# Squares of the scan's outputs made inside its last group, heads of z scaled ahead, and a held low half behind the gating

## The chip, the cores and the metric

The kernel runs on one core of a Trainium2 chip. The metric is device time in microseconds. The core's engines are TensorE (PE; its weight loads are shown apart as PEld), VectorE (DVE), ScalarE (ACT), GpSimd (POOL) and SyncE (SP). Each works through its own instructions in order, and they wait for each other on semaphores. SP issues all weight loads.

## The reference

The program is a chain of layers on 272 tokens (16 meta tokens and 256 of the input; 48 places of padding in front count for nothing). What matters here is the gated delta rule of the first layer, cut to its skeleton:

```python
qkv = silu(causal_conv(h @ w_in[:, :4096]))      # q and k: 8 heads of 128, v: 16 heads of 128
z = h @ w_in[:, 4096:6144]                       # 16 heads of 128
# chunkwise scan over the tokens, per head: o = S^T q, S decays and takes in k v^T
o = o * rsqrt(mean(o * o, -1) + eps) * norm_w    # one factor per head and token
o = o * silu(z)
mix = o.reshape(L, 2048) @ w_out
```

Behind it stand the layer's feed-forward network, a second layer (mLSTM and feed-forward), and a second block with attention over the tokens and over a memory; the change doesn't touch them.

## The kernel before

All activations are held with features on the 128 partitions and tokens along the row: a head is a tile of 128 x 272 floats. A product of the split kind is made of three fp32r matmuls for each block of 128 x 128 weights (`L432` high weights by high input, `L433` high by low, `L434` low by high). For this, each slab of weights (128 x 2048, 1 MB) in `ring` is taken apart into `w_hi`, a rounded copy by ACT (`L302`), and `w_lo`, the rest, by DVE (`L305`). `ring` has four slots, `w_hi` and `w_lo` two. ACT may round slab n + 2 when PE has finished slab n; DVE follows; then SP may load slab n + 6's place, the slot just emptied (the load of a slab waits for `w_lo` of the slab four before it). `each_product` writes these steps into the order of an engine: for the unit j of a phase it issues the split (`ahead`) for each slab that ends with this unit, then the unit's `body`, then `late` for unit j - lag; after the last unit it runs `late` for the remaining ones. With `end="hold"` the split of the last slab is left out there, and a call of `prepare` makes it later.

**The scan.** The 16 value heads are worked through in four groups of four, each with tokens in two chunks. A group is a chain of levels (l = 1 to 5, then a last one): PE multiplies 64 x 64 blocks, DVE masks and subtracts, ACT copies one product of each chunk (`L1366`, at the last level `L1371`). Then come values, state and outputs. ACT copies the outputs of chunk 1 (`o1`) and chunk 2 (`outputs(2)`, which counts `group_out`) into `qkv[:, 16:32, :]` (`L1383`). In the first three groups ACT, DVE, PE and POOL also make the next group's inputs between these steps; in the last group there are none. The rows that POOL fetches for the groups (`bc`) and the squares of the outputs (`osq`) lie in the same memory, so squares can be written only when POOL has done its work for the last group (`ahead_pool`).

**Between scan and z.** ACT waits for the whole scan (`scan_done`), squares all 16 heads with one instruction (`L609`), makes `w_hi` of z's first two slabs, and the high halves of the input in eight steps (`L483`). DVE makes the two `w_lo`, then the eight low halves (`L491`). PE sums the squares over the partitions in `rown_pe` (`L636`, 16 blocks, each a matmul with one column of ones; in fp32, so two passes each) and goes on with z. ACT takes the root (`L620`), DVE the reciprocal (`L625`), POOL writes the 16 rows to memory and reads them back on all partitions (`obc`, `L1523`, `L1525`).

**z.** 8 slabs with two units (heads) each. ACT: `Silu` of the product into one of four tiles `zs` (`L1531`), and four units later the high half of the gated head (`L1537`). DVE: two units behind the product, the scaling of the head with `obc` (`L1547`), its gating with `zs` (`L1550`), and from unit 5 on at odd units the low half of a pair of heads (`L1559`):

```python
if un.u % 2 and un.u >= 5:
    low(un.u // 2 - 2)
```

`low(6)` and `low(7)` stand behind the phase. `x_lo` counts the pairs, and PE, which starts `gdn_out` right behind z, waits for pair k // 2 before block k. `gdn_out` has 8 slabs of 16 blocks, one product each. Behind the last gate POOL fetches `mem0`, squares and sums it (`L1957`, `L1960`) for a product that PE makes ahead of slab 5 of `gdn_out`.

The semaphore `rown_squares` counts squares of three uses: 16 of the keys and queries, 1 for the outputs, 2 of the memory's.

Of the kernel before, what the change touches and what calls it, by code (L numbers as in the profile page):

```python
# [19 lines left out]
ALU = mybir.AluOpType  # L20
# [8 lines left out]
T = META + SEQ  # L29
TILES = [(0, META), (META, P), (META + P, P)]  # L30
HQ, HV = 8, 16
# [169 lines left out]
def program(nc, x_t, meta_t, mem_t, positions, stream, consts, params, sg_w_t, sg_bias, out_t, counts):  # L201
    with ExitStack() as ctx:
# [424 lines left out]
        def rown_pe(pe, use, sqr, blocks, per_row, n, rows):  # L627
            S.begin("rown_pe")
            if use == 3:
                pe.wait_ge(*S.at("mla_act", "ksq"))  # L630
            else:
                pe.wait_ge(S.sem("rown_squares"), (16, 17, 19)[use])
            for k in range(blocks):
                src = sqr(k)
                h = k // per_row
                mm = pe.matmul(ps[5 if use == 3 else 4][0:rows, 0:n], cn("row_of", 15 - h, rows)[0:src.shape[0], :], src,  # L636
                               start=(k == 0), stop=(k == blocks - 1))
            S.inc(mm, "rown_pe", "sums")
# [3 lines left out]
        qkv = area(0, 32, T)  # L642
# [711 lines left out]
        def nothing_more():  # L1354
            pass

        def group_act(act, g, last):
            inc = lambda ins, step=None: S.inc(ins, "scan_act", step)
            S.begin("scan_act")
            for c in CHUNKS:  # L1360
                ahead_values_act(act, g, c)
            for l in range(1, TOP):
                for c in CHUNKS:
                    act.wait_ge(*S.at("scan_pe", f"XT{c}.{l}", g))
                    if l < TOP - 1:
                        inc(act.activation(XT64[c], packed(bank(c, 1)), ACT.Copy), f"XT{c}.{l}")  # L1366
                    else:
                        if g == 0 and c == 1:
                            act.wait_ge(*S.at("first_zeros"))
                        for s in HALVES:  # L1370
                            inc(act.activation(buf[c]["XT"][s, :, s], packed(bank(c, 1))[s], ACT.Copy), f"XT{c}.{l}" if s.start else None)  # L1371
                if l in (3, 4) and not last:
                    ahead_exp(act, g + 1, l - 2)

            def new_values(c):
                act.wait_ge(*S.at("scan_pe", f"vn{c}", g))
                inc(act.activation(buf[c]["vn"], tile4(bank(c, 1)), ACT.Copy), f"vn{c}")

            def outputs(c):
                t0, n = TILES[c]  # L1380
                act.wait_ge(*S.at("scan_pe", f"o{c}", g))
                dst = work[:, 16 * T:32 * T].rearrange("p (g h t) -> p g h t", h=4, t=T)[:, g, :, t0:t0 + n]
                return act.activation(dst, tile4(bank(c, 2)), ACT.Copy)  # L1383
            new_values(1)
            inc(outputs(1), "o1")
            new_values(2)
            if not last:
                ahead_x_act(act, g + 1, 1)
            outputs(2).then_inc(S.sem("group_out"), 1)
            if not last:  # L1390
                ahead_x_act(act, g + 1, 2)
# [148 lines left out]
            each_product(act, "gdn_z", 1, body, split="hi", late=high, lag=4, turns=0)  # L1540

        def gate_dve(dve):
            def body(un):
                S.begin("gate_dve")
                dve.wait_ge(S.sem("o_rows_in"), 16)
                o = qkv[:, 16 + un.u, :]
                S.inc(dve.scalar_tensor_tensor(out=o, in0=o, scalar=pm("gdn_norm"), in1=obc[:, un.u, :], op0=ALU.mult, op1=ALU.mult), "gate_dve")  # L1547
                S.own(dve, "gate_dve", un.u + 4)
                un.was_read(dve)
                S.inc(dve.tensor_tensor(o, o, zs[:, un.j % 4, :], ALU.mult), "gate_dve")  # L1550
                if un.u % 2 and un.u >= 5:
# [2 lines left out]
            def low(pair):  # L1554
# [2 lines left out]
                dve.wait_ge(*S.at("x_hi", pair, 2))  # L1557
                k = slice(2 * pair, 2 * pair + 2)
                S.inc(dve.tensor_tensor(O_LO[:, k, :], qkv[:, 16 + 2 * pair:18 + 2 * pair, :], O_HI[:, k, :].bitcast(F32), ALU.subtract), "x_lo", pair)  # L1559
            each_product(dve, "gdn_z", 1, nothing, split="lo", late=body, lag=2, turns=0)  # L1560
            low(6)
            low(7)

# [1076 lines left out]
        def _(act):  # L2640
# [21 lines left out]
            act.wait_ge(*S.at("qkv_act", turn=31 + CONV_AHEAD))  # L2662
            scan_act(act)
            scan_done(act)
            rown_squares(act, [(qkv[:, 16:32, :], osq)])
            prepare(act, "hi", "gdn_z")
            split_act(act, 1, a, A_HI, 8, T)
            rown_act(act, 1, [], T, 16, 1.0 / P, cn("eps"))
# [77 lines left out]
        def _(dve):  # L2746
# [5 lines left out]
            dve.memset(raw_c[:, :, 0:3], 0.0).then_inc(S.sem("qkv_dve"), CONV_AHEAD * 3)  # L2752
            dve.memset(rs[:, 0, 16:20], 0.0).then_inc(S.sem("qkv_act"), CONV_AHEAD)
            dve.memset(rs[:, 0, 20:24], 0.0).then_inc(S.sem("up_dve"), 2 * 4)
            dve.memset(rs[:, 0, 32:36], 0.0).then_inc(S.sem("gate_dve"), 4 * 2)
            dve.memset(rs[:, 0, 36:40], 0.0).then_inc(S.sem("hid_pool"), 4 * 2)
            dve.memset(rs[:, 0, 24:28], 0.0).then_inc(S.sem("up_act"), 2)
            dve.memset(rs[:, 0, 28:32], 0.0).then_inc(S.sem("up_pool"), 2 * 3)
# [2 lines left out]
                dve.wait_ge(bank_free[i], 1)  # L2761
            dve.wait_ge(S.sem("up_pool"), 6)
            dve.wait_ge(S.sem("qkv_act"), CONV_AHEAD)
            dve.wait_ge(S.sem("gate_dve"), 8)
            dve.wait_ge(S.sem("hid_pool"), 8)
            dve.wait_ge(S.sem("up_act"), 2)
            dve.wait_ge(S.sem("up_dve"), 8)
# [23 lines left out]
            split_dve(dve, 1, a, A_HI, A_LO, 8, T)  # L2791
            rown_dve(dve, 1, T, 16)
            gate_dve(dve)
            each_product(dve, "gdn_out", 1, lambda un: mem_norm_dve(dve, un.j), turns=0, split="lo", end="hold")
            for layer in range(2):
                if layer:
# [69 lines left out]
        def _(pe):  # L2866
# [7 lines left out]
            def gates_block(k):  # L2874
# [8 lines left out]
                if k == DB - 1:  # L2883
# [6 lines left out]
            stream_pe(pe, "gdn_qkv", a_parts(0, T), T, lead=1, between=lambda slab: qkv_pe(pe, 2 * slab),  # L2890
                      inside=lambda slab, part: qkv_pe(pe, 2 * slab + part))
            scan_pe(pe)
            pe.wait_ge(S.sem("group_out"), GROUPS + 1)
            rown_pe(pe, 1, lambda k: osq[:, k, :], 16, 1, T, 16)
            stream_pe(pe, "gdn_z", a_parts(1, T), T)
            stream_pe(pe, "gdn_out", split_input(pe, O_HI, O_LO, T, by_step(pe, 2, per=2)), T,
                      between=lambda slab: mem_norm_pe(pe) if slab == 5 else None)
# [231 lines left out]
```

## Time and profile before

| | |
|---|---|
| median of 3 runs | 1634.16 us (1631.63 to 1638.73) |
| the profiled execution | 1625.85 us, its span 1624.0 us |
| PE busy | 1556.2 us (96%) |
| DVE, ACT, POOL busy | 1064.9, 798.7, 373.5 us |
| mean granted clock of TensorE | 0.987 |

The busy times are of the profiled execution. PE is nearly always busy, so the stretches in which it isn't, and what ended them, are what to look for; the granted clock is 1.00 at full speed and 0.50 at the lower level.

### The profile page before, as it was taken

The page shows a single profiled execution, that of the slowest core. Times are in us where ns is not written, and L with a number is a line of the kernel's source. Part 1 is how long each engine was busy: PE and PEld are TensorE (multiplying, and loading weights), DVE is VectorE, ACT ScalarE, POOL GpSimd, SP SyncE. Part 2 cuts the span into 40 slices and gives each one's busy share as a digit, 9 for nine tenths or more (in the row PEclk, how much of TensorE's full clock was granted, in tenths as well). Part 3 has the DMA queues.
Part 4 walks back from the last instruction along what each step waited for, and adds up shares of the span by engine and source line. Part 5 has one row for each costly group of instructions (what it writes and reads, how often), then busy time and mean ns, then how long its engine had stood idle before and what let it go on. Part 6 is the DMA issues. An engine that isn't in the chain of part 4 may idle for free.

```text
span 1624.0 us, 33710 instructions
## 1 busy us (share of the span) xinstructions
PE 1556.2 (96%) x13961; PEld 1476.5 (91%) x13961; DVE 1064.9 (66%) x1531; ACT 798.7 (49%) x1202; POOL 373.5 (23%) x387
## 2 busy tenths in 40 slices
PE   6999999889899999999999999999999898899998
PEld 6898988789899998988999999999996798899998
DVE  6785465474888736665888557665557665666653
ACT  7764333554555546545655554434444246364332
POOL 0014442006266520003366311220000000212110
PEclk9999999999999999999999999999999999999999
DMA  7463220354555455623454556545633532545553
GB/s 271 156 196 94 51 60 2 134 185 165 184 179 181 143 169 180 210 93 125 161 181 157 178 198 207 203 148 192 230 113 119 208 129 93 194 160 203 175 169 122
DMA packets 43373, 256.47 MB, mean 158 GB/s; under 512 B 5712, under 2 KB 7872, under 8 KB 20992
## 3 DMA queue, kind: packets, MB, share of 16 engines
q1 hardware_dynamic: 38704, 233.26, 41.9%
q0 software_dynamic: 4416, 20.60, 4.4%
q8 instruction: 81, 1.33, 0.3%
q10 hardware_dynamic: 144, 1.05, 0.2%
q14 instruction: 28, 0.23, 0.0%
HBM read 252.68 MB, written 2.22 MB: 157 GB/s over the span
## 4 chain that ended last, share of the span: by engine, by line
PE 77%; DVE 8%; issue 7%; ACT 5%; DMA 2%; POOL 0%; ACTq 0%; SPq 0%; DVEq 0%; POOLq 0%
PE bank L432 21%; PE bank L434 21%; PE bank L433 21%; PE bank L1259 3%; DVE w_lo L305 2%; ACT w_hi L302 2%; DMA sq<-rows_scratch_q 1%; ACT work L2490 1%; DVE rs L589 1%; PE bank L636 1%; DVE mix L595 1%; DVE w_spare L1332 1%; PE bank L1429 1%; PE bank L1421 0%; PE bank L1436 0%
## 5 line engine op out<-in xcount | busy, mean ns | idle before, releaser
L432 PE MATMUL bank<-work_r,w_hi 128*128 128x256 f32 (+2 forms) x3248 | 923.8, 284 | 16.7 <-DVE w_lo L305 6.7
L433 PE MATMUL bank<-work_r,w_hi 128*128 128x256 f32 (+2 forms) x3248 | 916.2, 282 | 0.0
L434 PE MATMUL bank<-work_r,w_lo 128*128 128x256 f32 (+2 forms) x3248 | 915.9, 282 | 0.0
L305 DVE TENSOR_TENSOR w_lo<-ring,w_hi 128x2048 fp32r<-128x2048 f32 (+2 forms) x233 | 499.7, 2145 | 320.7 <-ACT w_hi L302 320.6
L432 PEld LDWEIGHTS bank<-work_r,w_hi 128*128 128x128 f32 x3248 | 614.8, 189 | 30.1 <-issue 12.8
L302 ACT ACTIVATE w_hi<-ring 128x2048 fp32r<-128x2048 f32 (+2 forms) x233 | 408.5, 1754 | 459.7 <-PE bank L434 459.6
L434 PEld LDWEIGHTS bank<-work_r,w_lo 128*128 128x128 f32 x3248 | 615.1, 189 | 0.0
L433 PEld LDWEIGHTS bank<-work_r,w_hi 128*128 128x128 f32 x3248 | 614.7, 189 | 0.3
L1647 POOL TENSOR_TENSOR work<-work 128x272 f32<-128x272 f32 (+1 forms) x44 | 92.6, 2104 | 131.1 <-ACT work L1609 131.1
L1635 DVE SCALAR_TENSOR_TENSOR work<-work,params_sb 128x272 f32<-128x272 f32 (+1 forms) x176 | 99.6, 606 | 5.1 <-DVE work L1635 0.2
L545 POOL TENSOR_TENSOR sq<-sq 128x256 f32<-128x256 f32 (+2 forms) x36 | 53.6, 1488 | 177.8 <-ACT sq L521 176.8
L2044 POOL CAST work_r<-mix 128x256 f32 (+1 forms) x44 | 17.6, 399 | 185.3 <-DVE mix L2035 185.3
L845 DVE SCALAR_TENSOR_TENSOR work<-work,params_sb 128x272 f32<-128x272 f32 x96 | 49.6, 522 | 10.3 <-ACT work L812 8.1
L1623 DVE TENSOR_TENSOR work<-bank,rs 128x272 f32<-128x272 f32 (+1 forms) x88 | 37.7, 431 | 27.1 <-PE bank L434 27.0
L450 PE MATMUL bank<-work_r,w_hi 128*128 128x272 f32 (+2 forms) x128 | 42.8, 335 | 7.7 <-DVE work_r L2067 4.5
L1602 ACT ACTIVATE work<-work,params_sb 128x272 f32<-128x272 f32 (+1 forms) x88 | 48.2, 595 | 2.5 <-DVE work L1623 2.4
L2056 ACT ACTIVATE work_r<-hs,params_sb 128x256 fp32r<-128x256 f32 (+2 forms) x48 | 24.6, 513 | 45.1 <-DVE hs L2088 17.6
L1651 POOL TENSOR_TENSOR work_r<-work,work_r 128x272 f32 (+3 forms) x44 | 39.9, 908 | 7.7 <-POOL work_r L1649 7.3
L1332 DVE TENSOR_TENSOR w_spare<-bank,w_spare 128x256 f32<-128x256 f32 x40 | 16.6, 421 | 35.5 <-PE bank L1259 35.4
L2029 DVE TENSOR_TENSOR mix<-bank,rs 128x256 f32<-128x256 f32 x44 | 18.7, 425 | 30.8 <-PE bank L434 30.8
L2046 POOL TENSOR_TENSOR work_r<-mix,work_r 128x256 f32 (+1 forms) x44 | 35.6, 808 | 7.5 <-POOL work_r L2044 7.2
L2560 POOL TENSOR_TENSOR work<-work,mix 128x256 f32<-128x256 f32 x8 | 5.9, 739 | 135.4 <-DVE mix L2551 135.4
(450 smaller groups left out, 1713.6 us busy)
## 6 DMA issues: line engine op xcount, KB each, us to landing
ring<-in_stream SPq DMA_DIRECT2D x164, 1024.0 KB, 4.9
ring<-in_stream SPq DMA_DIRECT2D x64, 704.0 KB, 4.1
ring<-in_stream SPq DMA_DIRECT2D x10, 768.0 KB, 4.3
work<-rows_scratch POOLq DMA_DIRECT2D x12, 512.0 KB, 5.8
ring<-in_stream SPq DMA_DIRECT2D x7, 512.0 KB, 3.7
work<-mem_scratch POOLq DMA_DIRECT2D x3, 1024.0 KB, 5.0
work<-rows_scratch POOLq DMA_DIRECT2D x4, 544.0 KB, 6.0
work<-rows_scratch_o POOLq DMA_DIRECT2D x1, 2176.0 KB, 8.7
```

The source lines that it names most:

```text
L302: eng.activation(w_hi[:, slot, 0:size], raw_w, ACT.Copy).then_inc(hi_done, 1)
L305: eng.tensor_tensor(w_lo[:, slot, 0:size], raw_w, w_hi[:, slot, 0:size].bitcast(F32), ALU.subtract).then_inc(lo_done, 1)
L432: pe.matmul(out, w_hi[:, slot, at:at + P], hi, start=first, stop=False)
L433: pe.matmul(out, w_hi[:, slot, at:at + P], lo, start=False, stop=False)
L434: mm = pe.matmul(out, w_lo[:, slot, at:at + P], hi, start=False, stop=last)
L450: pe.matmul(out, w_hi[:, slot, at:at + P], hi, start=(k == 0), stop=False)
L545: S.inc(pool.tensor_tensor(sq[:, 0, 0:n], sq[:, 0, 0:n], sq[:, k, 0:n], ALU.add), "square_sums")
L845: S.inc(dve.scalar_tensor_tensor(out=y, in0=r[:, t:t + T], scalar=gdn_taps[:, un.u, t:t + 1], in1=y, op0=ALU.mult, op1=ALU.add), "qkv_dve")
L1259: mm = pe.matmul(out[s, side(h)], left[s, h, :], right[s, h, :], start=True, stop=True)
L1602: S.inc(act.activation(y_gu[p2][:, m, 0:w], raw[p2][:, m, 2:w + 2], ACT.Identity, bias=bias[:, un.u, m:m + 1], scale=taps[:, un.u, m, 2:3] ...
L1635: S.inc(dve.scalar_tensor_tensor(out=y, in0=raw[p2][:, m, t:t + w], scalar=taps[:, un.u, m, t:t + 1], in1=y, op0=ALU.mult, op1=ALU.add), " ...
L1647: S.inc(pool.tensor_tensor(h, silu_g[un.j % 2][:, 0:w], y_gu[un.j % 2][:, 1, 0:w], ALU.mult), "up_pool")
```

## The change

The squares of groups 0, 1 and 2 are made by ACT in the last group, one group's (4 x 272 elements) behind the copies of each of levels 2, 3 and 4. Ahead of the first ACT waits for POOL's work for the last group. Only the last group's squares stand behind the scan. `rown_squares` now counts four for this use; `rown_pe` waits for three ahead of block 0 and for the fourth ahead of block 12, and stands ahead of PE's wait for `group_out`.

In z, DVE scales heads ahead of their gating from unit 8 on: unit 8 scales heads 8 and 9, unit 9 head 10, unit 10 heads 11 and 12, unit 11 head 13, unit 12 heads 14 and 15. A semaphore `head_scaled` counts them, and `gate_dve` now counts the gates alone. The `w_lo` of slab 1 of `gdn_out`, which stood in z's last unit, is held until `low(7)` is issued.

```diff
--- before.py
+++ after.py
@@ -629,8 +629,10 @@
             if use == 3:
                 pe.wait_ge(*S.at("mla_act", "ksq"))
             else:
-                pe.wait_ge(S.sem("rown_squares"), (16, 17, 19)[use])
+                pe.wait_ge(S.sem("rown_squares"), (16, 19, 22)[use])
             for k in range(blocks):
+                if use == 1 and k == blocks - 4:
+                    pe.wait_ge(S.sem("rown_squares"), 20)
                 src = sqr(k)
                 h = k // per_row
                 mm = pe.matmul(ps[5 if use == 3 else 4][0:rows, 0:n], cn("row_of", 15 - h, rows)[0:src.shape[0], :], src,
@@ -1354,6 +1356,9 @@
         def nothing_more():
             pass
 
+        def output_squares(act, g):
+            rown_squares(act, [(qkv[:, 16 + 4 * g:20 + 4 * g, :], osq[:, 4 * g:4 * g + 4, :])])
+
         def group_act(act, g, last):
             inc = lambda ins, step=None: S.inc(ins, "scan_act", step)
             S.begin("scan_act")
@@ -1371,6 +1376,12 @@
                             inc(act.activation(buf[c]["XT"][s, :, s], packed(bank(c, 1))[s], ACT.Copy), f"XT{c}.{l}" if s.start else None)
                 if l in (3, 4) and not last:
                     ahead_exp(act, g + 1, l - 2)
+                if l in (2, 3, 4) and last:
+                    if l == 2:
+                        act.wait_ge(*S.at("ahead_pool", turn=GROUPS - 1))
+                    act.wait_ge(*S.at("scan_act", "o1", l - 2))
+                    act.wait_ge(S.sem("group_out"), l)
+                    output_squares(act, l - 2)
 
             def new_values(c):
                 act.wait_ge(*S.at("scan_pe", f"vn{c}", g))
@@ -1540,12 +1551,18 @@
             each_product(act, "gdn_z", 1, body, split="hi", late=high, lag=4, turns=0)
 
         def gate_dve(dve):
+            scaled = []
+
             def body(un):
                 S.begin("gate_dve")
                 dve.wait_ge(S.sem("o_rows_in"), 16)
+                upto = un.u + 1 if un.u < 8 else min(HV, un.u + 1 + (un.u - 6) // 2)
+                for h in range(len(scaled), upto):
+                    x = qkv[:, 16 + h, :]
+                    S.inc(dve.scalar_tensor_tensor(out=x, in0=x, scalar=pm("gdn_norm"), in1=obc[:, h, :], op0=ALU.mult, op1=ALU.mult), "head_scaled")
+                    scaled.append(h)
+                dve.wait_ge(S.sem("head_scaled"), un.u + 1)
                 o = qkv[:, 16 + un.u, :]
-                S.inc(dve.scalar_tensor_tensor(out=o, in0=o, scalar=pm("gdn_norm"), in1=obc[:, un.u, :], op0=ALU.mult, op1=ALU.mult), "gate_dve")
-                S.own(dve, "gate_dve", un.u + 4)
                 un.was_read(dve)
                 S.inc(dve.tensor_tensor(o, o, zs[:, un.j % 4, :], ALU.mult), "gate_dve")
                 if un.u % 2 and un.u >= 5:
@@ -1557,7 +1574,7 @@
                 dve.wait_ge(*S.at("x_hi", pair, 2))
                 k = slice(2 * pair, 2 * pair + 2)
                 S.inc(dve.tensor_tensor(O_LO[:, k, :], qkv[:, 16 + 2 * pair:18 + 2 * pair, :], O_HI[:, k, :].bitcast(F32), ALU.subtract), "x_lo", pair)
-            each_product(dve, "gdn_z", 1, nothing, split="lo", late=body, lag=2, turns=0)
+            each_product(dve, "gdn_z", 1, nothing, split="lo", late=body, lag=2, turns=0, end="hold")
             low(6)
             low(7)
 
@@ -2662,7 +2679,7 @@
             act.wait_ge(*S.at("qkv_act", turn=31 + CONV_AHEAD))
             scan_act(act)
             scan_done(act)
-            rown_squares(act, [(qkv[:, 16:32, :], osq)])
+            output_squares(act, GROUPS - 1)
             prepare(act, "hi", "gdn_z")
             split_act(act, 1, a, A_HI, 8, T)
             rown_act(act, 1, [], T, 16, 1.0 / P, cn("eps"))
@@ -2752,7 +2769,7 @@
             dve.memset(raw_c[:, :, 0:3], 0.0).then_inc(S.sem("qkv_dve"), CONV_AHEAD * 3)
             dve.memset(rs[:, 0, 16:20], 0.0).then_inc(S.sem("qkv_act"), CONV_AHEAD)
             dve.memset(rs[:, 0, 20:24], 0.0).then_inc(S.sem("up_dve"), 2 * 4)
-            dve.memset(rs[:, 0, 32:36], 0.0).then_inc(S.sem("gate_dve"), 4 * 2)
+            dve.memset(rs[:, 0, 32:36], 0.0).then_inc(S.sem("gate_dve"), 4)
             dve.memset(rs[:, 0, 36:40], 0.0).then_inc(S.sem("hid_pool"), 4 * 2)
             dve.memset(rs[:, 0, 24:28], 0.0).then_inc(S.sem("up_act"), 2)
             dve.memset(rs[:, 0, 28:32], 0.0).then_inc(S.sem("up_pool"), 2 * 3)
@@ -2761,7 +2778,7 @@
                 dve.wait_ge(bank_free[i], 1)
             dve.wait_ge(S.sem("up_pool"), 6)
             dve.wait_ge(S.sem("qkv_act"), CONV_AHEAD)
-            dve.wait_ge(S.sem("gate_dve"), 8)
+            dve.wait_ge(S.sem("gate_dve"), 4)
             dve.wait_ge(S.sem("hid_pool"), 8)
             dve.wait_ge(S.sem("up_act"), 2)
             dve.wait_ge(S.sem("up_dve"), 8)
@@ -2791,6 +2808,7 @@
             split_dve(dve, 1, a, A_HI, A_LO, 8, T)
             rown_dve(dve, 1, T, 16)
             gate_dve(dve)
+            prepare(dve, "lo", "gdn_out")
             each_product(dve, "gdn_out", 1, lambda un: mem_norm_dve(dve, un.j), turns=0, split="lo", end="hold")
             for layer in range(2):
                 if layer:
@@ -2890,8 +2908,8 @@
             stream_pe(pe, "gdn_qkv", a_parts(0, T), T, lead=1, between=lambda slab: qkv_pe(pe, 2 * slab),
                       inside=lambda slab, part: qkv_pe(pe, 2 * slab + part))
             scan_pe(pe)
+            rown_pe(pe, 1, lambda k: osq[:, k, :], 16, 1, T, 16)
             pe.wait_ge(S.sem("group_out"), GROUPS + 1)
-            rown_pe(pe, 1, lambda k: osq[:, k, :], 16, 1, T, 16)
             stream_pe(pe, "gdn_z", a_parts(1, T), T)
             stream_pe(pe, "gdn_out", split_input(pe, O_HI, O_LO, T, by_step(pe, 2, per=2)), T,
                       between=lambda slab: mem_norm_pe(pe) if slab == 5 else None)
```

## Rows read from the trace of the kernel before

**Rows 1.** The page's first line: span and instructions.
```profile
span 1624.0 us, 33710 instructions
```

**Rows 2.** Waits of PE, whole run: total us, times, longest us.
```profile
PE bank L432 <- DVE w_lo L305: 6.7, 11, 1.5
...
PE bank L636 <- ACT work L609: 4.6, 1, 4.6
...
PE bank L432 <- DVE work_r L1559: 4.3, 2, 2.9
```

**Rows 3.** Timeline 290 to 312: start us, us, engine, line, what, [idle before <- releaser].
```profile
293.60 0.60 ACT L1383 ACTIVATE work<-bank 128x512 f32<-128x512 f32 x1 [1.25 <-PE bank L1441]
294.23 3.83 ACT L609 ACTIVATE work<-work 128x4352 f32<-128x4352 f32 x1
297.96 3.69 ACT L302 ACTIVATE w_hi<-ring 128x2048 fp32r<-128x2048 f32 x2
...
298.20 8.87 PE L636 MATMUL bank<-work,consts_sb 128*16 128x272 f32 x32 [4.64 <-ACT work L609]
...
300.88 5.67 PEld L636 LDWEIGHTS bank<-work,consts_sb 128*16 128x16 f32 x25 [0.30 <-issue]
...
304.30 2.90 DVE L491 TENSOR_TENSOR work_r<-a,work_r 128x272 fp32r<-128x272 f32 x8
...
307.00 0.40 PE L432 MATMUL bank<-work_r,w_hi 128*128 128x272 f32 x1
...
307.62 1.84 DVE L625 RECIPROCAL rrow<-rrow 16x272 f32<-16x272 f32 x1 [0.42 <-ACT rrow L620]
```

**Rows 4.** Windows: us, busy of each engine, PEclk, DMA share, GB/s.
```profile
298.20:299.50 1.30, 1.30 (x3) 0.41 (x4) 0.00 (x0) 1.30 (x1) 0.00 (x0) 0.50 0.00 0
...
424.00:428.20 4.20, 2.92 (x19) 2.33 (x17) 2.58 (x3) 3.03 (x3) 0.00 (x0) 1.00 0.07 27
```

**Rows 5.** Timeline of PE, the seam.
```profile
362.99 0.59 PE L432 MATMUL bank<-work_r,w_hi 128*128 128x272 f32 x1 [1.40 <-DVE work_r L1559]
...
366.64 0.29 PE L432 MATMUL bank<-work_r,w_hi 128*128 128x272 f32 x1
```

**Rows 6.** Timeline of ACT, last group's levels.
```profile
274.92 0.39 ACT L1366 ACTIVATE w_spare<-bank 128x256 f32<-128x256 f32 x1 [1.76 <-PE bank L1259]
```

**Rows 7.** Timeline of DVE, first head of z.
```profile
321.02 0.50 DVE L1547 SCALAR_TENSOR_TENSOR work<-work,params_sb 128x272 f32<-128x272 f32 x1 [3.48 <-DMA work<-rows_scratch_o]
...
321.92 2.29 DVE L305 TENSOR_TENSOR w_lo<-ring,w_hi 128x2048 fp32r<-128x2048 f32 x1
```

**Rows 8.** Timeline of PE, z's slab 3.
```profile
324.88 0.28 PE L432 MATMUL bank<-work_r,w_hi 128*128 128x272 f32 x1
```

**Rows 9.** DMA queues from 312 to 319.5: packets, MB, share of 16 engines.
```profile
q0 software_dynamic: 119, 2.07, 77.4%
```

**Rows 10.** Timeline of SP from 312 to 319.
```profile
317.57 0.33 SPq L2603 DMA_DIRECT2D ring<-in_stream  x1
```

**Rows 11.** DMA queues from 319.5 to 320.2.
```profile
q0 software_dynamic: 17, 0.16, 53.7%
q1 hardware_dynamic: 8, 0.07, 50.6%
```

**Rows 12.** Timeline of DVE, the seam.
```profile
354.51 0.50 DVE L1547 SCALAR_TENSOR_TENSOR work<-work,params_sb 128x272 f32<-128x272 f32 x1
...
356.69 2.29 DVE L305 TENSOR_TENSOR w_lo<-ring,w_hi 128x2048 fp32r<-128x2048 f32 x1 [1.22 <-ACT w_hi L302]
...
362.21 1.99 DVE L1559 TENSOR_TENSOR work_r<-work,work_r 128x544 fp32r<-128x544 f32 x3
```

**Rows 13.** Timeline of ACT, the seam.
```profile
356.57 0.38 ACT L1531 ACTIVATE sq<-bank 128x272 f32<-128x272 f32 x1
...
359.91 0.43 ACT L1537 ACTIVATE work_r<-work 128x272 fp32r<-128x272 f32 x1 [2.33 <-DVE work L1550]
```

**Rows 14.** Timeline of POOL behind z.
```profile
375.52 9.50 POOL L1960 TENSOR_TENSOR work<-work 128x256 f32<-128x256 f32 x7
```

## The prediction

> **What bounds the kernel now.** I read the page first: TensorE (PE) is busy for 1556.2 of 1624.0 us [rows 1], so only time in which PE waits, or runs at the lower clock, can be won back. The next view is the table of whom PE waited for. Two of its waits belong to the edited code: 4.6 us in front of the row sums `L636`, for the big square `L609`, and 4.3 us in two pieces in front of `L432`, for the low parts of z's gated heads, `L1559` [rows 2]. The third row there, 6.7 us in 11 waits for `w_lo`, is what a cured wait can turn into.
>
> Then the timeline, stretch by stretch. At the end of the scan ACT copies the last output until 294.20 and squares all 16 heads in one instruction of 3.83 us. Only at 298.20 does PE start the 32 passes of the row sums; it needs 8.87 us and starts z at 307.00 [rows 3]. The windows show why 8.87: the granted clock is 0.50, the lower of TensorE's two levels, in the first passes [rows 4]; the later ones start twice as fast. At the seam between z and `gdn_out`, PE runs out of input, gets blocks 8 and 9, stands again until 362.99, restarts at the lower clock (0.23 us between starts against 0.13 later) and reaches slab 1 of `gdn_out` at 366.64 [rows 5]. I count the seam at this last moment, since all of `gdn_out` hangs on it.
>
> **Part one: squares in the last group's levels.** It removes nothing from ACT but moves three quarters of the square. A square of 4 x 272 elements lies between two rows: 0.60 us for 512 elements and 3.83 for 4352 [rows 3], so 0.84 ns for one more element, and 1088 give 0.60 + 576 x 0.00084 = 1.08 us. Three of these go into levels 2, 3 and 4, each behind the copy for chunk 2. There ACT is idle for 1.76 us before the next level's copy [rows 6], so 1.08 fits with 0.6 to spare, and it costs nothing. Bounds: at 0.96 (a quarter of 3.83) it fits still better; were the cover gone, three levels would pay 1.08 each, 3.2 us. The added waits (all of GpSimd's preparation of the last group, output copies of earlier groups) are for work that was over before level 2 began.
>
> Behind the last output one square of 1.08 remains in place of 3.83: ACT's `w_hi` and everything behind it start 2.75 us earlier. The row sums don't wait even for that: twelve blocks hang on squares long made, and PE can go on from 293.6, where the scan's last matmuls end. At the full clock a pass takes 5.67/25 = 0.227 us (25 weight loads from 300.88) [rows 3], 32 take 7.3, so they end at 300.9. The squares of the last group are there at 295.3, before block 12 is reached at 299. The gap of 4.6 us and the 1.6 us of slow clock are gone.
>
> But z needs `w_lo` of slab 0 and then the low part of its input, and these hang on ACT: two `w_lo` before ended at 304.30, when the first of eight `L491` began [rows 3]. Less 2.75 that is 301.55, the first block is ready at 301.9, z starts at 302.0: **5.0 us earlier** than 307.00. PE uses blocks at 0.37 us (three matmuls), DVE makes them at 0.36, so no wait follows inside.
>
> What is late next: the factors of the heads. The reciprocal `L625` stood at 307.62 behind the root. Now it stands behind DVE's last low part, at 307.20 - 2.75 = 304.45, that is only 3.17 earlier. It goes out to memory and comes back on all partitions, and the first head is scaled 13.40 us after the reciprocal's start (321.02 less 307.62) [rows 3, 7]: 317.85 now. DVE keeps its order there: scale and gate head 0 (0.90 us to the start of what follows), then `w_lo` of slab 3 (2.29) [rows 7]. Without collision this `w_lo` ends at 321.05. PE would want slab 3 17.88 us after z's start (its first matmul, the 145th of z, stood at 324.88 [rows 8]; less 307.00), at 319.9. So PE waits 1.2 us and starts slab 3 at 321.15, 0.1 behind its `w_lo`; of the 5.0 some 3.7 stay.
>
> There is also a collision. The copy on all partitions (2.23 MB) was nearly alone: 2.07 MB had moved by 319.5, and no packet of the weights' queue [rows 9]. The weight load that follows `w_lo` of slab 2 was issued at 317.57 [rows 10]. It hangs on PE's slab 0, which moves by 5.0, while the copy moves by 3.17: it comes 1.8 us earlier against the copy, and about 0.8 MB are then still to move. Where both queues ran, q0 got 0.16 MB in 0.7 us, 0.23 MB a us [rows 11]; 0.8 MB then take 3.5 us where they took 2.3, a delay of 1.2. The Trainium skill says (DMA: Bandwidth & Descriptors, "Queues, rings and completion order") that an engine turns from queue to queue at packet boundaries. The copy's packets being twice as large as the weights', by that rule the copy would get two thirds of the bytes, its delay would be 0.6, and z would keep 3.1. Bounds from rows alone are 0 and 1.2; I take 0.9, as only the first third of the weight load's bytes fall into it. **Part one: 3.7 - 0.9 = 2.8 us** (2.5 to 3.7; 5.0 if the copy never binds).
>
> **Part two: scales ahead, and the held `w_lo`.** I work in old times; all are shifted by part one alike. Scaling is not cheaper: 16 scales of 0.50 us in both. Heads 8 to 15 are only scaled earlier, in DVE's idle 1.2 us before each `w_lo` [rows 12]. Before, DVE waited there for ACT until 356.69, made `w_lo` of `gdn_out`'s slab 1 (2.29 us), and only then three heads and four low parts, until 364.2. Now from 354.51: two scales 1.0, gates of heads 12 and 13 at 0.40 (0.90 less 0.50), low part 4 at 0.66 (1.99/3), two gates, low parts 5, 6, 7. With all of them full length this ends at 359.74; starts overlap by some hundredths, so I take 359.6. Gate 15 needs ACT's curve for head 15, which stands behind `w_hi` and ends at 356.95 [rows 13], ahead of the 357.3 at which DVE comes to it. ACT's high parts follow each gate by 0.43 us while DVE is still at the pair before. PE wants block 10 at about 358.4; low part 5 ends at 358.2 to 358.4. So the 2.9 and 1.4 us stands go, and with them the slow clock (13 starts at 0.23 in place of 0.13, 1.3 us). Slab 0 of `gdn_out` ends at about 360.7.
>
> The price is the held `w_lo`: 359.6 + 2.29 = 361.9, PE starts slab 1 at 362.0 in place of 360.7, a new wait of 1.3 us. **Part two: 366.64 - 362.0 = 4.6 us** (4.3 if each step is 0.05 longer, 5.0 if overlaps are larger). The other lines: `memset`s and semaphore counts, nothing.
>
> **What follows.** The memory's input is fetched behind the last gate, 4.5 us earlier than before by part two, so its POOL chain, done at 385.02 before [rows 14], stays ahead of slab 5 of `gdn_out`, which came four slabs of 48 x 0.126 us behind 366.64, at 390.8; the 5.8 us between them hardly change. The rest of the program moves as a block.
>
> **Sum.** 2.8 + 4.6 = 7.4 us. The profiled execution took 1625.85 around its span of 1624.0 [rows 1]; 1618.45 is expected of its like. The median of the runs shown is 1634.16, so 1626.8. This is 0.45%, and half a per cent (8.2 us) is about what a measurement here tells from no change.
>
> **The rivals.**
> (a) The copy doesn't bind: the DMA chain is shorter under another load, and the path over `w_lo` of slab 3 isn't last. Then 5.0 + 4.6 to 5.0, 9.8 us, 1624.4. For it: only 1.1 us of computed lateness; against it: the order of DVE's queue, which holds slab 3's `w_lo` behind head 0. With smaller collisions it runs into the forecast. Chance 0.17.
> (b) The seam keeps its length: low part 7 doesn't end before about 363 because each gate and high part wait for each other between ACT and DVE, and `w_lo` behind them then ends at 365.3 or later. Only the slow clock's part is won: 2.8 + 1.3 = 4.1 us, 1630.1. For it: in the old trace each of the last gates cost a round trip, ACT idle for 2.33 us in front of a high part [rows 13]; against it: the scales that made it are away. Chance 0.12.
> (c) The clock falls in the new short stands (2 us at slab 3, 1.3 at slab 1). Against it: between 424.0 and 428.2 PE was busy for 2.92 of 4.2 us and stayed at 1.00 [rows 4]. Price 1.3 each, 2.6: 4.8 us left, 1629.4. Chance 0.10.
> (d) The other side: slower. The same mechanism further down: every stand after the scan comes 7.4 us earlier, and the clock falls in those in which it had held. At 1.3 us each six of the 11 waits for `w_lo` [rows 2] cancel the gain; if all 11 and both new ones lost it, 13 x 1.3 = 16.9, net 9.5 us slower, 1643.7. Nothing in the windows speaks for it. Chance 0.03.
> The forecast itself (6 to 9.5 us) has 0.58.
>
> **Range and chances.** The likeliest is 1626.8, its own range 1624.7 to 1628.2. The runs of before lie within 7.1 us of each other, so a median can be off by 3 without any cause; with (a) at the low end and (b), (c) at the high end: 1621.5 to 1632.0. Faster by over 0.5% needs 8.2 us: all of (a) and a quarter to a third of the forecast's weight with the measurement's spread, 0.42. Slower 0.03. The rest, 0.55, is within 0.5%.
>
> **What would show it.** Right: no PE gap between the last scan matmul and `L636`, its passes all at 0.23 us, z about 5 us earlier, a wait of 1 to 2.5 us for `w_lo` at slab 3 of z, no wait for `L1559`, one of about 1.3 us for `w_lo` at slab 1 of `gdn_out`. Wrong: longer gaps in the levels of the last group, slab 3 without a wait (then a), or waits for low parts at the seam (then b).

## The result

The changed kernel took 1621.84 us (median of 6 runs, 1616.81 to 1624.66) against 1632.13 us of the kernel before (6 runs, 1629.17 to 1638.73): ratio 0.993, 95% interval 0.9907 to 0.9952. It is faster by 0.7%, where 0.45% was forecast and "within half a per cent" had the largest chance. The profiled execution has a span of 1618.4 us (1624.0 in [rows 1]), that is only 5.6 us less; why the medians lie 10.3 apart and the two spans 5.6 is a question of its own, taken up below. (A stand, in what follows, is a stretch in which PE is idle because it waits.)

The table of PE's waits, whole run (total us, times, longest us). The row for `L609` and the one for `L1559` [rows 2] are gone; waits for `w_lo` went from 11 with 6.7 us to 12 with 9.8. `L491` made PE wait once before, for 5.3 us in another phase; now it does so twice, and the new wait is the 1.17 us at z's start:

```profile
PE bank L432 <- DVE w_lo L305: 9.8, 12, 1.5
PE bank L432 <- DVE work_r L491: 6.3, 2, 5.1
```

PE's timeline behind the scan. Against [rows 3] the last output copy stands 1.27 us later (294.87, in ACT's rows further down), and so does the one of the group before (265.26 against 263.99): the last group takes 29.61 us in both, so the delay lies ahead of the change, and I measure from the last output copy ("slab 3 at 28.06" is 28.06 us behind its start). In the old trace the row sums began at 4.60, now they begin 0.11 us ahead of the copy, and take 7.51 us in place of 8.87:

```profile
294.76 7.51 PE L638 MATMUL bank<-work,consts_sb 128*16 128x272 f32 x32
```

PE's gaps in z and at the seam. z starts 8.57 us behind the last output copy (13.40 before). Slab 3 waits for its `w_lo`, and so does slab 1 of `gdn_out`, the last row, which stood at 366.64 in [rows 5]:

```profile
303.44 0.36 PE L432 MATMUL bank<-work_r,w_hi 128*128 128x272 f32 x1 [1.17 <-DVE work_r L491]
...
322.93 0.39 PE L432 MATMUL bank<-work_r,w_hi 128*128 128x272 f32 x1 [1.49 <-DVE w_lo L305]
...
358.61 0.29 PE L434 MATMUL bank<-work_r,w_lo 128*128 128x272 f32 x1
359.84 0.39 PE L432 MATMUL bank<-work_r,w_hi 128*128 128x272 f32 x1 [0.94 <-DVE w_lo L305]
```

DVE's timeline at the first head and at the seam, for [rows 7, 12]. Read the seam (the passage from z to `gdn_out`) as one chain without a gap: two scales (x2), gates 12 and 13, low part 4, gates 14 and 15, low parts 5 to 7, the held `w_lo`:

```profile
305.67 1.83 DVE L625 RECIPROCAL rrow<-rrow 16x272 f32<-16x272 f32 x1
...
319.69 0.50 DVE L1562 SCALAR_TENSOR_TENSOR work<-work,params_sb 128x272 f32<-128x272 f32 x1 [5.76 <-DMA work<-rows_scratch_o]
...
320.59 2.29 DVE L305 TENSOR_TENSOR w_lo<-ring,w_hi 128x2048 fp32r<-128x2048 f32 x1
...
352.54 0.91 DVE L1562 SCALAR_TENSOR_TENSOR work<-work,params_sb 128x272 f32<-128x272 f32 x2
353.37 0.79 DVE L1567 TENSOR_TENSOR work<-work,sq 128x272 f32<-128x272 f32 x2
354.07 0.72 DVE L1576 TENSOR_TENSOR work_r<-work,work_r 128x544 fp32r<-128x544 f32 x1
354.70 0.97 DVE L1567 TENSOR_TENSOR work<-work,sq 128x272 f32<-128x272 f32 x2
355.59 1.99 DVE L1576 TENSOR_TENSOR work_r<-work,work_r 128x544 fp32r<-128x544 f32 x3
357.50 2.28 DVE L305 TENSOR_TENSOR w_lo<-ring,w_hi 128x2048 fp32r<-128x2048 f32 x1
```

ACT's timeline in the last group's levels, for [rows 6], and at the end of the scan: the square of 1.10 us sits in the pause, and the copy behind it still waits 0.76 us for PE; the last output copy is followed by the one square that is left:

```profile
274.04 0.38 ACT L1371 ACTIVATE w_spare<-bank 128x256 f32<-128x256 f32 x1 [0.55 <-PE bank L1261]
274.32 1.10 ACT L609 ACTIVATE work<-work 128x1088 f32<-128x1088 f32 x1
276.19 0.38 ACT L1371 ACTIVATE w_spare<-bank 128x256 f32<-128x256 f32 x1 [0.76 <-PE bank L1261]
...
294.87 0.60 ACT L1394 ACTIVATE work<-bank 128x512 f32<-128x512 f32 x1 [1.25 <-PE bank L1452]
295.50 1.11 ACT L609 ACTIVATE work<-work 128x1088 f32<-128x1088 f32 x1
```

### The profile page after: what moved, and what is told of

The parts are those of the page before. It is cut to its first block, busy times and chain, and to the rows that moved or that the text cites. A ratio compares the mean times of both kernels' runs of the same rounds, so it can differ in the third digit from the quotient of the medians.

```text
span 1618.4 us, 33715 instructions
## 1 busy us (share of the span) xinstructions
PE 1555.4 (96%) x13961; PEld 1477.3 (91%) x13961; DVE 1063.1 (66%) x1531; ACT 798.6 (49%) x1205; POOL 372.7 (23%) x387
## 4 chain that ended last, share of the span: by engine, by line
PE 62%; issue 6%; DVE 5%; ACT 3%; DMA 1%; POOL 0%; ACTq 0%; DVEq 0%; POOLq 0%
PE bank L432 19%; PE bank L434 19%; PE bank L433 19%; DVE w_lo L305 2%; ACT w_hi L302 1%; DMA sq<-rows_scratch_q 1%; ACT work L2507 1%; DVE mix L595 1%; DVE rs L589 0%; PE bank L580 0%; PE bank L450 0%; PE bank L451 0%; PE bank L452 0%; PE bank L1837 0%; PE bank L2441 0%
## 5 line engine op out<-in xcount | busy, mean ns | idle before, releaser
L847 DVE SCALAR_TENSOR_TENSOR work<-work,params_sb 128x272 f32<-128x272 f32 x96 | 49.6, 523 | 10.3 <-ACT work L814 8.1
L1334 DVE TENSOR_TENSOR w_spare<-bank,w_spare 128x256 f32<-128x256 f32 x40 | 16.6, 421 | 36.8 <-PE bank L1261 36.7
```

What stands on the lines that cost most here:

```text
L847: S.inc(dve.scalar_tensor_tensor(out=y, in0=r[:, t:t + T], scalar=gdn_taps[:, un.u, t:t + 1], in1=y, op0=ALU.mult, op1=ALU.add), "qkv_dve")
```

## The experiments

All distances below are from the start of the last output copy to the start of a PE row; z's slab 3 and slab 1 of `gdn_out` are the marks. In the kernel before they are 324.88 - 293.60 = 31.28 and 366.64 - 293.60 = 73.04 us, in the changed one 28.06 and 64.97.

**Both kernels again.** No edit.

> The kernel before, unchanged, timed against itself. Both theories expect a ratio of 1.000. It shows how far two medians of the same program lie apart, and its trace shows whether the execution profiled before (1625.85 us, while the six timed runs lay between 1629.17 and 1638.73) was a typical one. If only the clock's falls differ from run to run, the stretch from the last output copy of the scan to slab 1 of gdn_out is again 73.0 us within 0.5, and the total differs elsewhere.

> The changed kernel again. Theory 'local': the change wins 8.1 us between the last output copy and slab 1 of gdn_out (73.04 to 64.97 us in the two traces) and nothing else; ratio 0.9951, between 0.993 and 0.997. Theory 'more than local': about 3 us more are won outside that stretch because the clock falls less often there; ratio 0.993 again, and the stretches outside are shorter in the traces of the changed kernel than in those of the one before.

Before against itself: ratio 0.9986 (0.9964 to 1.0009), span 1629.3. The changed kernel: 0.994 (0.9917 to 0.9964), span 1624.5, slab 3 at 27.68 and slab 1 at 64.58. Slab 3 and slab 1 of the kernel before stood at 31.23 and 72.95. The local stretch repeats within 0.4 us in both, while the spans of the same program differ by 5.3 and 6.1. So one profiled span against another says little on a change of 8 us, but the stretch around the change says it within half a microsecond: 8.1 and 8.5 us against the first trace of before. Both intervals of the timed runs hold 0.995, which 8.1 to 8.5 us would give, and both reach further down. "More than local" is not shown by any stretch of a trace and not shut out by the intervals: some 2 us of the 10.3 between the medians stay without a place.

**Part one alone.**

```diff
# of the change: rown_pe, group_act, output_squares, the order in front of z
-            rown_squares(act, [(qkv[:, 16:32, :], osq)])
+            output_squares(act, GROUPS - 1)
# gate_dve, its semaphores and prepare(dve, "lo", "gdn_out") as before
```

> Part one alone: squares of three groups in the last group's levels, row sums ahead of the wait for the whole scan; the seam as before. My term, corrected by the trace of after: z's slab 3 starts 3.2 us earlier against the last output copy (31.28 us before, 28.06 after), and all behind it likewise; ratio 0.998. Rival (the parts lean on each other: the old seam gives part of it back, since its low halves hang on DVE and not on PE): under 2 us at slab 1 of gdn_out.

Ratio 0.9975 (0.9953 to 0.9996). PE's gaps:

```profile
302.31 0.37 PE L432 MATMUL bank<-work_r,w_hi 128*128 128x272 f32 x1 [1.16 <-DVE work_r L491]
...
321.53 0.39 PE L432 MATMUL bank<-work_r,w_hi 128*128 128x272 f32 x1 [1.21 <-DVE w_lo L305]
...
357.32 0.39 PE L432 MATMUL bank<-work_r,w_hi 128*128 128x272 f32 x1 [2.90 <-DVE work_r L1570]
...
359.73 0.60 PE L432 MATMUL bank<-work_r,w_hi 128*128 128x272 f32 x1 [1.39 <-DVE work_r L1570]
```

The last output copy started at 293.75, so z starts at 8.56, slab 3 at 27.78, 3.5 us earlier than before, and slab 1 of `gdn_out` at 69.63, 3.4 us earlier. The two waits at the seam are as long as in [rows 2], 2.90 and 1.39 against 2.9 and the rest of 4.3, only all earlier by 3.4: at most 0.1 us of part one is given back.

**Part two alone.**

```diff
# of the change: gate_dve, end="hold", prepare(dve, "lo", "gdn_out"), counts of gate_dve
# squares in one instruction behind the scan, rown_pe behind group_out, as before
```

> Part two alone: heads scaled one to three ahead and the w_lo of slab 1 of gdn_out held behind low(7); squares as before. Additive theory: 4.9 us, from z's slab 3 to slab 1 of gdn_out 36.9 us in place of 41.8, ratio 0.997. Rival: the gain at the seam needs part one, under 3 us.

Ratio 0.9973 (0.9953 to 0.9994). Slab 1 starts at 68.91 us, 4.1 earlier. But in this execution the clock rose later inside the row sums (ten weight loads 0.45 us apart, against six in the trace of before), so z began 0.8 late. From z's slab 3 on (0.8 later, at 32.11) it is 36.8 us against 41.76: 4.9 us, as expected. The parts add: 3.5 + 4.9 = 8.4, and 0.9975 x 0.9973 = 0.9948.

**Hold and scales apart.**

```diff
# scales_no_hold: heads scaled ahead, w_lo of slab 1 of gdn_out in z's last unit
-            each_product(dve, "gdn_z", 1, nothing, split="lo", late=body, lag=2, turns=0, end="hold")
+            each_product(dve, "gdn_z", 1, nothing, split="lo", late=body, lag=2, turns=0)
# hold_no_scales: w_lo held, each head scaled in its own unit
-                upto = un.u + 1 if un.u < 8 else min(HV, un.u + 1 + (un.u - 6) // 2)
+                upto = un.u + 1
```

> The changed kernel with the w_lo of slab 1 of gdn_out back in z's last unit; heads still scaled ahead. If the hold carries the seam: DVE waits for w_hi again (until about 356.7 in old times), and the gates of heads 13 to 15 and four low parts follow its 2.3 us; low part 7 ends near 362.9, and PE reaches slab 1 about 2.5 to 4 us later than in the changed kernel. If the scales carry it: under 1 us later, since w_lo then is ready early and needn't be waited for.

> The changed kernel with each head scaled in its own unit again; w_lo of slab 1 still held. Against the changed kernel two scales (heads 14 and 15 and head 13, 0.41 to 0.53 us each) come back into DVE's last chain, so low part 7 and w_lo end 0.5 to 1.1 us later and so does PE's slab 1. Rival (the scales matter most): 2 us or more later.

Each of the two is one execution. Without the hold PE stands twice for low halves, as in the old seam but shorter (slab 1 follows slab 0 at once, at 66.61):

```profile
354.62 0.39 PE L432 MATMUL bank<-work_r,w_hi 128*128 128x272 f32 x1 [2.36 <-DVE work_r L1576]
...
355.96 0.39 PE L432 MATMUL bank<-work_r,w_hi 128*128 128x272 f32 x1 [0.32 <-DVE work_r L1576]
```

Slab 1 at 66.61 is 2.0 us later than the 64.58 of the changed kernel's second trace, which had the same slab 3 (27.64 and 27.68): a little under the range I gave for the hold, well above 1. Without the scales slab 1 is at 65.72, slab 3 at 27.55: 38.17 us between them against 36.9, so the scales are worth 1.3 us behind the hold, a little over the range. Measured from slab 3 the scales alone take 38.97 us and the hold alone 38.17, against 41.76 before. So of the 4.9 us that both give together, the hold alone gives 3.6 and the scales alone 2.8: 1.5 us of it either one would win.

**The collision.** One load is held back, until the heads' factors have arrived. One execution.

```diff
+                if n == PLAN["gdn_z"].slab0 + 6:
+                    sp.wait_ge(S.sem("o_rows_in"), 16)
                 sp.dma_start(ring[:, n % SLOTS, 0:size], src)...
```

> The changed kernel, with the one weight load that follows w_lo of z's slab 2 held until the heads' factors have arrived (the load's data are needed some 20 us later). It takes the collision away. If the collision costs what I put on it, reciprocal's start to first scaled head falls from 14.02 us to 13.1 (before: 13.40, with the last 1.5 us shared), and slab 3 of z starts 0.5 to 0.9 us earlier. Rival: the copy isn't slowed by the load, no change beyond 0.2 us, and 14.02 against 13.40 comes from the copy itself.

The factors' way has two legs, the rows' way out to memory and the copy back on all partitions, and they must be looked at apart. From the issue of the copy on all partitions to the first scaled head it took 8.72 us in the old trace (312.30 to 321.02) and 9.45 in the changed kernel (310.24 to 319.69); here 8.86:

```profile
309.79 0.55 POOL L1534 DMA_DIRECT2D rows_scratch_o<-rrow  x1 [43.49 <-DVE rrow L625]
312.33 0.57 POOL L1536 DMA_DIRECT2D work<-rows_scratch_o  x1 [1.99 <-DMA rows_scratch_o<-rrow]
```

```profile
307.66 1.83 DVE L625 RECIPROCAL rrow<-rrow 16x272 f32<-16x272 f32 x1
...
321.19 0.50 DVE L1562 SCALAR_TENSOR_TENSOR work<-work,params_sb 128x272 f32<-128x272 f32 x1 [5.26 <-DMA work<-rows_scratch_o]
```

The other leg, the rows' way out, takes 2.0 to 2.5 us without a pattern in all these executions (2.54 here, 2.44 and 2.05 in the changed kernel's). So the copy took 0.6 us less with the load away. The other traces bear this out, with a spread of 0.3: where the load was issued 3.7 to 4.2 us behind the copy, the copy took 9.38 to 9.47 us (five executions); at 4.8 us behind it took 9.20; at 5.3 us and later, or held back, 8.69 to 9.00 (four). The sum of both legs moved only from 14.02 to 13.53 and would have misled: my figure of 13.1 forgot the first leg's spread.

At PE little of it arrives: slab 3 starts at 27.56 and slab 1 at 64.46, only 0.1 to 0.5 us earlier than in the changed kernel's two traces, where I had expected 0.5 to 0.9; with the load in place the kernel without scales had its slab 3 at 27.55. Here the rows' way out was at the long end of its range and hid part of the gain.

How the load slows the copy stays open. It was issued at 313.96 in the changed kernel, but none of its packets starts before 318.0; the first do so in the half microsecond in which the copy's last eight full ones start. Queues from 314 to 318, then from 318 to 318.5, then from 318.5 to 319:

```profile
q0 software_dynamic: 72, 1.25, 87.2%
```

```profile
q0 software_dynamic: 8, 0.14, 74.4%
q1 hardware_dynamic: 6, 0.05, 23.6%
```

```profile
q1 hardware_dynamic: 17, 0.14, 66.0%
q0 software_dynamic: 8, 0.00, 0.9%
```

The prediction's 0.6 by the Trainium skill's rule (DMA: Bandwidth & Descriptors, "Queues, rings and completion order": turns at packet boundaries) is the number measured, but these rows show no turns between the two queues while the copy runs, so they don't bear the rule out as its cause.

**One step moved on DVE: `w_lo` of z's slab 3 first.**

```diff
+                if un.u == 0:
+                    first.append(un)
+                    return
+                if un.u == 1:
+                    gate(first[0])
+                gate(un)
```

> The changed kernel with one step moved: w_lo of z's slab 3 stands ahead of the first head's scaling and gating on DVE. If the order on DVE is what lets the copy reach PE, PE's wait of 1.49 us at slab 3 is gone and everything behind comes about 1.5 us earlier: 1.5 us faster than the changed kernel. Rival: PE then waits as long for a bank, since ACT's curve of head 4 waits for the first gate; no gain.

PE has no wait left at slab 3, and slab 1 of `gdn_out` starts at 63.20, 1.4 to 1.8 us earlier than in the changed kernel. No bank's wait takes its place. In the timed runs it doesn't show: 0.9944 (0.9925 to 0.9964).

**An earlier start of z, and both steps.**

```diff
-            prepare(act, "hi", "gdn_z")
+            prepare_one(act, "hi", "gdn_z")
             split_act(act, 1, a, A_HI, 8, T)
+            prepare(act, "hi", "gdn_z")
# the same on DVE around split_dve
```

> The changed kernel with z's input halves made before the second slab's w_hi (ACT) and w_lo (DVE) instead of behind them. PE no longer waits 1.16 us for the first low half, so z starts about 1.1 us earlier against the last output copy (8.57 to about 7.4). If the heads' copy on all partitions and DVE's order behind it bound z at slab 3, as part one's sum has it, slab 3 starts where it did (27.7 to 28.1, within 0.3) and the 1.1 us turn into a longer wait there. Rival: slab 3 comes 1.1 us earlier too.

> The step of the kernel before this one together with w_lo of z's slab 3 ahead of the first head. Both waits are away, so their gains add: slab 1 of gdn_out 2.6 us earlier than in the changed kernel (64.6 to 65.0 becomes about 62.2), some 10.5 us against the kernel before; ratio 0.9935 within the interval's 0.002. Rival: a bank's wait for the curve of head 4, which needs the first gate, takes part of it.

Both expectations were wrong, in direction too, and this was the most instructive pair (`input_first` is one execution). z did start without a wait, at 7.33. But slab 3 came at 29.50, 1.4 to 1.8 us later than in the changed kernel, after a wait of 4.14 us, and PE restarted at the lower clock (granted 0.50 from 324.5 to 328.5):

```profile
324.55 0.59 PE L437 MATMUL bank<-work_r,w_hi 128*128 128x272 f32 x1 [4.14 <-DVE w_lo L305]
```

```profile
307.97 0.55 POOL L1539 DMA_DIRECT2D rows_scratch_o<-rrow  x1 [43.48 <-DVE rrow L630]
311.32 0.56 POOL L1541 DMA_DIRECT2D work<-rows_scratch_o  x1 [2.80 <-DMA rows_scratch_o<-rrow]
```

The second weight load of z, which follows the second `w_lo`, is now issued at 305.95, right before the rows go out at 307.97; that leg took 3.35 us in place of 2.0 to 2.5. From 308 to 310 the weights' queue is nearly full (in the changed kernel its load is over by then, 10 packets from 308 to 312):

```profile
q1 hardware_dynamic: 102, 0.80, 95.1%
```

The next load is earlier as well, 1.62 us behind the copy's issue in place of 3.7, and the copy took 10.0 (311.32 to 321.32). Slab 1 starts at 68.70: behind slab 3 another 2.3 us are lost (39.20 us between them against 36.91), with the clock low. No run holds these loads back here, so that they are what slowed both legs is argued from the order of the issues. With `w_lo` of slab 3 first, the copy meets a further load and takes 11.7 us (312.15 to 323.86); slab 3 doesn't wait, but a wait of 2.77 us appears at slab 4, with the clock at 0.50 behind it (330 to 334), and slab 1 is at 67.76, 2.8 to 3.2 later than in the changed kernel. Timed: 0.9942 (0.9922 to 0.9963), not to be told from the others, as 3 us is 0.2%.

**Row sums that wait for all squares.**

```diff
-                pe.wait_ge(S.sem("rown_squares"), (16, 19, 22)[use])
+                pe.wait_ge(S.sem("rown_squares"), (16, 20, 22)[use])
```

> The changed kernel with the row sums waiting for all four squares instead of three. The last square ends 1.74 us after the last output copy starts, PE is free 0.1 us before that start: the sums begin 1.8 us later, at about 1.8, and end 7.3 us on, at 9.1 (at the lower clock later still); z then starts at about 9.1 in place of 8.57 but slab 3, bound by the copy, is at most 0.3 us later. If it is so, the twelve early blocks are worth next to nothing, and what counts is that the square of three groups is out of ACT's way.

The sums start at 1.79, as expected. z starts at 9.23, 0.7 us later. But the first head comes 0.3 to 0.7 us earlier (24.15), slab 3 starts at 27.39 with a gap of 0.3 us left in front of it, and slab 1 at 64.29, even 0.3 to 0.7 us before the changed kernel's (one execution). So in the changed kernel the early start of the sums buys nothing: what z meets at slab 3 is the copy's end, and the weight load, issued at 19.79 in place of 19.09, now troubles the copy less (9.20 us in place of 9.45). Together with `w_lo` first:

> The two single steps that came out best in the traces, together: w_lo of z's slab 3 ahead of the first head, and the row sums waiting for all four squares (z about 0.7 us later, so that its weight load falls less into the copy). If the copy's collision is what an earlier z pays for, slab 1 of gdn_out starts at about 63 to 64 us behind the last output copy, like the kernel with w_lo first alone (63.20), so a later start of z costs at most its own 0.7. Rival: both gains add, 62.6 or less. In the timed runs neither can be told from the changed kernel: ratio 0.994, interval about 0.002 each way.

63.89, that is the 63.20 of `w_lo` first plus 0.7 for the later z: with the copy out of PE's way the early sums do count. Timed: 0.9956 (0.9938 to 0.9974).

| kernel | slab 3 of z | slab 1 of gdn_out | ratio (interval) |
|---|---|---|---|
| before | 31.28 | 73.04 | |
| before, again | 31.23 | 72.95 | 0.9986 (0.9964 to 1.0009) |
| changed | 28.06 | 64.97 | 0.993 (0.9907 to 0.9952) |
| changed, again | 27.68 | 64.58 | 0.994 (0.9917 to 0.9964) |
| part one alone | 27.78 | 69.63 | 0.9975 (0.9953 to 0.9996) |
| part two alone | 32.11 | 68.91 | 0.9973 (0.9953 to 0.9994) |
| scales, no hold | 27.64 | 66.61 | one execution |
| hold, no scales | 27.55 | 65.72 | one execution |
| load behind the copy | 27.56 | 64.46 | one execution |
| input first | 29.50 | 68.70 | one execution |
| sums wait | 27.39 | 64.29 | one execution |
| `w_lo` of slab 3 first | no wait | 63.20 | 0.9944 (0.9925 to 0.9964) |
| same, input first | no wait (wait at slab 4) | 67.76 | 0.9942 (0.9922 to 0.9963) |
| same, sums wait | no wait | 63.89 | 0.9956 (0.9938 to 0.9974) |

Both marks are starts of PE's rows: slab 3 is the 145th matmul of z, slab 1 of `gdn_out` the 433rd behind z's start. The first row's trace is the one of [rows 1].

## Why the prediction was right and wrong

*Squares beside the levels*: right. 1.10 us each against 1.08, in a pause of 1.76, and the last group takes 29.61 us in both kernels.

*Row sums at once and at the full clock, z bound by its low halves*: right. Sums from -0.11 for 7.51 us, z at 8.57 where 302.0 - 293.60 = 8.4 was forecast. What I didn't see is that in this kernel the early sums are worth nothing by themselves: made to wait, they left slab 1 no later (64.29).

*Factors late, slab 3 waits*: right in mechanism and place, wrong in size. Reciprocal at 10.80 (forecast 10.85); slab 3 at 28.06 and 27.68 where 28.45 was forecast. The term that failed is the collision, put at 0.9. The copy took 0.7 us more than in the trace of before and 0.6 more than with the load held back; the rest of the distance to 28.45 is the rows' way out, 2.44 and 2.05 us in place of the 2.55 that stood in the trace of before and that I carried over as fixed. The bound of 1.2 had no ground: I took 0.23 MB a us from [rows 11] as the copy's rate beside a load, but the copy has 128 full packets, 119 of them in [rows 9], so that the 17 of those rows are its last 9 and 8 all but empty ones: the rate fell because the copy was ending. Nor does the 0.6 "by that rule" follow: two thirds of the bytes make 2.3 us into 3.45, a delay of 1.15, not 0.6. That 0.6 was measured is luck. Part one measured 3.2 to 3.6 us for 2.8.

*Scales and hold*: right in mechanism, a little small. No wait for low halves, full clock, one wait for `w_lo` of 0.94 us (1.3 forecast). The chain on DVE was shorter than I made it: gates in a row start 0.36 us apart, not 0.40, and the second of two scales 0.41 behind the first, not 0.50. Part two measured 4.9 for 4.6.

*The sum and its chances*: this is where the prediction failed. The local sum of 7.4 us was too small: 8.1 to 8.5 were won, 0.4 to 0.8 of the difference in part one (collision and way out) and 0.2 to 0.3 in part two (DVE's chain, where I had the starts in the trace and took the durations). The bound to "faster" that I had set was 8.2. A forecast 0.8 us under it, with both its soft terms rounded to the cautious side, was no ground for 0.55 on "within"; and its own parts, all of (a) and a quarter to a third of 0.58, make 0.31 to 0.36 for "faster", not 0.42. The forecast of 1626.8 also stands on a median of three runs, 2.0 us above that of all six. From the six it would have been 1624.7, 2.9 above the measured 1621.84. Of these 2.9, 0.7 to 1.1 are the terms above. The rest, some 2 us, I can't give a place: no stretch of a trace shows it, the kernel timed against itself gave 0.9986, and it may be spread, so that the timed result lies beyond half a per cent may be luck in part.

*Rivals*: (a) no: PE waits at slab 3 behind the copy and the first head, and with `w_lo` moved ahead of them the wait is gone. (b) no. (d) no. (c) no, the clock was 1.00 behind the stands of 1.49 and 0.94 us. It was 0.50 behind the 4.14 and the 2.77 us of the two kernels with their input first, so the rival's mechanism exists, for stands longer than the changed kernel has. Windows view behind the stands, the changed kernel and the one with its input first (columns as in [rows 4]):

```profile
322.90:324.00 1.10, 1.07 (x8) 1.07 (x9) 1.06 (x3) 0.69 (x2) 0.00 (x0) 1.00 0.24 30
359.80:361.00 1.20, 1.16 (x9) 1.17 (x10) 0.06 (x1) 1.20 (x2) 0.00 (x0) 1.00 1.09 362
```

```profile
324.50:328.50 4.00, 3.95 (x17) 3.95 (x18) 3.93 (x6) 1.12 (x3) 0.00 (x0) 0.50 0.76 250
```

## What to carry to other kernels

When an early part of a phase is pulled forward, look at what transfer stands in the path behind it and which loads move with the compute: here one of z's weight loads, moved forward with it, cost the copy that z itself waited for 0.6 us, and a still earlier start of z made the stretch 3.7 to 4.1 us longer. Measure a change of a few us by the distance between two marks around it in the traces, not by the spans. And when a forecast lands close to the bound between two verdicts, give both nearly the same chance.

## What the runs showed of the hardware

The same program's looped phases ran at one of two paces. In `up2`, PE is busy without a gap in every trace, the clock is 1.00, and in the same 105 us it made 927 to 929 matmuls in nine of the fourteen traces and 893 or 894 in the other five. Windows view of the changed kernel's two traces (columns as in [rows 4]):

```profile
1000.00:1080.00 80.00, 80.00 (x709) 80.00 (x708) 53.20 (x61) 32.57 (x30) 16.39 (x29) 1.00 0.53 177
```

```profile
1000.00:1080.00 80.00, 80.00 (x681) 80.00 (x681) 51.20 (x57) 31.88 (x29) 16.35 (x29) 1.00 0.53 181
```

The starts of matmuls are 0.113 us apart in one and 0.118 in the other. Missing rows don't explain it: between the same two of ACT's weight roundings around `up2` (969.85 and 1119.63 in the changed kernel) the nine traces took 149.2 to 150.0 us and the five 153.9, some 4 to 4.7 us more. `up3` did the same in other traces (936 or 937 matmuls in 110 us in two traces, before again among them, 968 to 973 in the rest; some 4 us). One such phase is worth about half of what the change wins, and it makes 4.1 of the 6.1 us between the changed kernel's two spans. What sets the pace I don't know; no wait, no DVE or ACT row explains it, and nothing here was tried on it. Beside it stands the clock's rise and fall, which varies ahead of the change: between 140 and 165 us its mean was 0.85 in the old trace, 0.80 and 0.73 in the changed kernel's two, and the last output copy started anywhere from 291.73 to 301.41 us in the fourteen executions, at no clear relation to the edits.
